# A GeGLU feed-forward by seven block products per pair of tiles, its down sums and residual rows in DRAM, and row-tiled state products in HGRN2

## What is computed

```python
h = rms_norm(x, norm_mix_pre)
proj = h @ w_in + b_in                      # 2048 x 11272
y_a = hgrn2_mix(...)                        # gated linear recurrence, 8 heads of 128, chunks of 64
y_b = mlstm_mix(...)                        # matrix memory, 4 heads
merged = sigmoid(gate_a) * (y_a @ w_up_a) + sigmoid(gate_b) * (y_b @ w_up_b)
x = x + rms_norm(merged @ w_out, norm_mix_post)
h = rms_norm(x, norm_ffn_pre)
gate = causal_dwconv(h @ ffn_w_gate, ffn_conv_w, ffn_conv_b)     # 2048 x 5632, three taps in time
up = h @ ffn_w_up                                                # 2048 x 5632
ffn_out = (gelu(gate, approximate=True) * up) @ ffn_w_down       # 5632 x 2048
x = x + rms_norm(ffn_out, norm_ffn_post)
```

## Time and profile before

| | |
|---|---|
| median of 3 runs | 2930.51 us (2930.03 to 2930.74) |
| the profiled execution | 2930.79 us, span of its core 2929.1 us |
| PE / PEld / DVE / ACT / POOL busy | 2886.0 / 2399.9 / 1149.2 / 823.2 / 87.8 us |
| granted TensorE clock | 0.996 of 2.4 GHz in the mean |
| DMA | 309 MB, mean 106 GB/s |

### The profile page before, as it was taken

The page is one execution under the profiler, slowest core; times in us unless marked ns, Lnnn a source line. Parts: engine busy times, 40 slices in busy tenths (PEclk is TensorE's granted clock), DMA queues, the critical chain, the costliest instruction groups (busy, mean ns, idle before and its releaser), DMA issues.

```text
span 2929.1 us, 32534 instructions
## 1 busy us (share of the span) xinstructions
PE 2886.0 (99%) x13167; PEld 2399.9 (82%) x13167; DVE 1149.2 (39%) x1141; ACT 823.2 (28%) x741; POOL 87.8 (3%) x99
## 2 busy tenths in 40 slices
PE   7999999999999999999999999999999999999997
PEld 6888888888888888888888888888888888888886
DVE  4232343344333234432554343343434343443436
ACT  3243434332222222222432222222221222122224
POOL 1000001000000000000000000000000000000004
PEclk9999999999999999999999999999999999999999
DMA  4323223332332334434333332333233233323334
GB/s 182 89 87 111 86 90 96 109 100 86 101 90 83 99 94 155 138 129 172 129 90 97 101 100 86 100 100 94 92 100 100 92 94 100 100 91 95 100 94 165
DMA packets 402657, 309.16 MB, mean 106 GB/s; under 512 B 5662, under 2 KB 349858, under 8 KB 401072
## 3 DMA queue, kind: packets, MB, share of 16 engines
q1 hardware_dynamic: 393824, 283.13, 31.0%
q0 software_dynamic: 4176, 16.95, 1.6%
q10 hardware_dynamic: 4608, 8.39, 0.7%
HBM read 295.87 MB, written 12.58 MB: 105 GB/s over the span
## 4 chain that ended last, share of the span: by engine, by line
PE 95%; DVE 2%; ACT 1%; POOL 1%; issue 0%; DMA 0%; DVEq 0%; SPq 0%; ACTq 0%
PE ps L657 21%; PE ps L386 18%; PE ps L660 11%; PE ps L389 9%; PE ps L405 7%; PE ps L407 7%; PE ps L406 7%; PE ps L603 6%; PE ps L679 1%; PE ps L678 1%; PE ps L677 1%; DVE w_lo L1126 1%; ACT w_hi L707 0%; PE ps L623 0%; DVE arena L1147 0%; PE ps L522 0%
## 5 line engine op out<-in xcount | busy, mean ns | idle before, releaser
L1126 DVE TENSOR_TENSOR w_lo<-raw,w_hi 128x2048 fp32r<-128x2048 f32 x260 | 597.1, 2297 | 1031.5 <-ACT w_hi L707 1031.5
L707 ACT CAST w_hi<-raw 128x2048 fp32r<-128x2048 f32 x260 | 496.3, 1909 | 615.9 <-PE ps L407 483.0
L657 PE MATMUL ps<-h_hi,w_hi 128*128 128x512 f32 x1376 | 325.9, 389 | 0.0
L657 PE MATMUL ps<-h_lo,w_hi 128*128 128x512 f32 x1376 | 325.9, 389 | 0.0
L660 PE MATMUL ps<-h_hi,w_lo 128*128 128x512 f32 x1376 | 325.9, 389 | 0.0
L657 PEld LDWEIGHTS ps<-h_lo,w_hi 128*128 128x128 f32 x1376 | 258.3, 188 | 53.6
L660 PEld LDWEIGHTS ps<-h_hi,w_lo 128*128 128x128 f32 x1376 | 258.3, 188 | 53.6
L657 PEld LDWEIGHTS ps<-h_hi,w_hi 128*128 128x128 f32 x1376 | 258.2, 188 | 53.6
L386 PE MATMUL ps<-h_hi,w_hi 128*128 128x512 f32 x1152 | 281.2, 397 | 1.1 <-ACT w_hi L707 1.1
L389 PE MATMUL ps<-h_hi,w_lo 128*128 128x512 f32 x1152 | 272.8, 389 | 0.0
L386 PE MATMUL ps<-h_lo,w_hi 128*128 128x512 f32 x1152 | 272.8, 389 | 0.0
(11 more groups left out here) (259 smaller groups left out, 2468.9 us busy)
## 6 DMA issues: line engine op xcount, KB each, us to landing
raw<-in_w_in SPq DMA_DIRECT2D x88, 1024.0 KB, 5.0
raw<-in_ffn_w_down SPq DMA_DIRECT2D x48, 1024.0 KB, 4.9
raw<-in_ffn_w_gate SPq DMA_DIRECT2D x44, 1024.0 KB, 5.1
raw<-in_ffn_w_up SPq DMA_DIRECT2D x44, 1024.0 KB, 5.1
raw<-in_w_out SPq DMA_DIRECT2D x20, 1024.0 KB, 4.9
merge_gates<-arena ACTq DMA_DIRECT2D x32, 256.0 KB, 2.0
raw<-in_w_up_a SPq DMA_DIRECT2D x8, 1024.0 KB, 5.0
raw<-in_w_up_b SPq DMA_DIRECT2D x8, 1024.0 KB, 5.1
```

What stands on the lines that cost most here:

```text
L657: pe.matmul(ps[:, bank + s, :], w[0][:, j, :], k[:, j, :], start=(k is h_hi and j == 0), stop=False)
L707: act.copy(w_hi[:, s, :], raw[:, s, :]).then_inc(hi_ready, 1)
L1126: dve.tensor_tensor(w_lo[:, s, :], raw[:, s, :], f32(w_hi[:, s, :]), ALU.subtract).then_inc(lo_ready, 1)
```

## The change

**Gate and up.** The weight of two hidden tiles (256 units x 2048 inputs) is cut into four quarters of 128 units x 1024 inputs: A11, A12 (first tile; first and second half of the inputs), A21, A22. h is cut into four quarters of 1024 inputs x 256 tokens. Instead of eight quarter products, seven products of sums (Strassen) are made, in the order M4, M2, M3, M5, M1, M7, M6. Four of the weight operands are new sums made on POOL (`weight_sum`: A21+A22, A11+A12, A11+A22, A12-A22, each 128x1024), one on DVE (`sum6`: A21-A11). All seven operands are then split into hi (ACT) and lo (DVE), each 128x1024, into a ring of three (`op_ring`). The seven operands of h are made once, ahead of the feed-forward: sums of token rows on DVE and POOL, 14 groups of 8 transposes (`turn_pieces`), and their split straight out of PSUM (`pieces_hi`, `pieces_lo`, 128x1024). In them hi and lo of 256 tokens stand side by side, so that one matmul of 512 columns makes w_hi*h_hi and w_hi*h_lo, and one of 256 columns w_lo*h_hi (`product`: 8 + 8 matmuls). Per pair of tiles the results are combined out of PSUM: three copies on ACT (`keep_product`), six additions of 128x512 on DVE (`with_m2` to `with_m6`, `from_m1`), four of 128x256 that join the two column halves (`both_halves`). The first tap moves from DVE to ACT.

**Loads.** Quarters of 512 KB go into a ring of six (`quad_ring`); a down block is two of them (`down(i, d, 0)` and `(i, d, 1)`, 24 matmuls each).

**Down sums.** The sums over the steps no longer lie in SBUF. ACT copies each 128x512 block out of PSUM (`down_copy`), and POOL issues a DMA that adds it to the tensor `down_sums` in DRAM (16 a step, `accum_op`; the first step writes). They are loaded back before the last down projection. `x1` too is stored to DRAM and loaded back for the last addition. The last step keeps the split of all its eight down operands for both halves of the tokens, where before the second half loaded and split them again.

**HGRN2.** The transposed keys of the two chunks lie in the two row halves of one tile (`hg_ket`, one copy on ACT in place of two, no zeroed padding), and the two state updates are matmuls over 64 rows each, issued in turns.

The core of the diff:

```diff
-            with pe.Fori(0, TT) as i:
+            for i in range(TT):
...
-                pe.wait_ge(k_end_copied, 2 * i + 2)
+                pe.wait_ge(k_end_copied, i + 1)
+                pe.wait_ge(hg_scores_copied, 2 * i + 2)
                 for h in range(HG_H):
-                    mm = pe.matmul(hT_[:, h, :], ke0[:, h, :], v_hg[:, ds(i, 1), h * P:(h + 1) * P], start=True, stop=True)
-                mm.then_inc(hg_update0, 1)
+                    m0 = pe.matmul(hT_[:, h, :], ket[0:CHUNK, h, :], v_hg[0:CHUNK, i:i + 1, h * P:(h + 1) * P],
+                                   start=True, stop=True)
+                    m1 = pe.matmul(hA_[:, h, :], ket[CHUNK:P, h, :], v_hg[CHUNK:P, i:i + 1, h * P:(h + 1) * P],
+                                   start=True, stop=True)
+                m0.then_inc(hg_update0, 1)
...
+            def product(i, p, q):
...
+                pe.wait_ge(ff_hi, o + 1)
+                for j in range(HALF):
+                    pe.matmul(ps[:, bank, :], w[0][:, j, :], h[:, j, :, :].rearrange("p r t -> p (r t)"),
+                              start=(j == 0 and q not in (M7, M6)), stop=False, skip_group_check=True)
+                pe.wait_ge(ff_lo, o + 1)
+                for j in range(HALF):
+                    mm = pe.matmul(ps[:, bank, 0:TH], w[1][:, j, :], h[:, j, 0, :], start=False, stop=(j == HALF - 1),
+                                   skip_group_check=True)
+                mm.then_inc(ff_op, 1)
...
+            def weight_sum(i, p, q):
...
+                if q == M2 or q == M5:
+                    before = o - PRODUCTS if p else o - OPS + 3 * PRODUCTS
+                    past(pool, ff_lo, before + (M1 if q == M2 else M7) + 1)
+                else:
+                    pool.wait_ge(ff_lo, o + (M2 if q == M1 else M5) + 1)
+                pool.tensor_tensor(dst, quads[(4 * p + a) % QRING], quads[(4 * p + b) % QRING],
+                                   ALU.subtract if q == M7 else ALU.add).then_inc(ff_sum, 1)
+
+            def sum_down(i, d, first):
+                for n in range(TT):
+                    pool.wait_ge(dn_evac, 16 * i + 4 * d + n + 1)
...
+                        pool.dma_start(dst, src, accum_op=ALU.add).then_inc(acc_added[n], 16)
...
+            def interval(i, k, with_lo=True):
...
+                if q == M2:
+                    with_m2(i, p)
+                elif q == M3:
+                    both_halves(i, p, X4)
+                    sum6(i, p)
+                elif q == M5:
+                    with_m5(i, p)
+                    both_halves(i, p, X3)
+                elif q == M7:
+                    with_m7(i, p)
+                    both_halves(i, p, X1)
+                    if up:
+                        times_gate(i, p, 0)
+                elif q == M6:
+                    with_m6(i, p)
+                    both_halves(i, p, Y2)
+                    if up:
+                        times_gate(i, p, 1)
+                    else:
+                        taps(i, p, 0)
+                    if p == 3:
+                        hidden_lo(i, p, 1)
+                if with_lo:
+                    lo(i, k + 2)
+                if q == M1:
+                    from_m1(i, p)
+                elif q == M7 and up:
+                    hidden_lo(i, p, 0)
+                elif q == M6 and p == 1:
+                    hidden_lo(i, p, 1)
+                elif q == M4 and up:
+                    taps(i, p - 1, 1)
```

More of the change, by code:

```diff
@@ L628, in _ @@
             for half, tiles in enumerate(HALVES):
                 for q in range(4):
+                    if half == 1 and q == 3:
+                        for r in range(4):
+                            turn_pieces(r)
                     u = U_OUT + 12 + 4 * half + q
@@ new lines, in ff_step, with need @@
+            def ff_step(i):
+                for p in range(PAIRS):
+                    for q in range(PRODUCTS):
+                        product(i, p, q)
+                for d in range(4):
+                    for h in range(2):
+                        down(i, d, h)
+            def need(count):
+                pe.wait_ge(th_lo, count)
+            need(2)
+            product(0, 0, M4)
+            need(4)
+            product(0, 0, M2)
+            for r in range(4, 8):
+                turn_pieces(r)
@@ L1078, in _, with row_power @@
             pool.dma_start(g_pre2, row_on_all(norm_ffn_pre, 0, D)).then_inc(x2_loaded, 16)
[L1080 removed]
+            def row_power(what, n):
                 if what == "mix":
@@ new lines, in _ @@
+            for n in range(2):
+                dve.tensor_tensor(x_rows[:, 2 + n, LEFT], x_rows[:, n, LEFT], x_rows[:, 2 + n, LEFT], ALU.add).then_inc(h_diff, 1)
+            lo(0, 5)
+            pieces_lo(10)
+            pieces_lo(11)
+            with_m5(0, 0)
+            dve.wait_ge(h_pool, 5)
+            dve.wait_ge(turned2, 8)
+            sum6(0, 0)
+            lo(0, 6)
+            pieces_lo(12)
+            lo(0, 7)
+            from_m1(0, 0)
+            pieces_lo(13)
+            both_halves(0, 0, X4)
```

796 lines of the change are left out of this document (577 added, 219 removed).

## The result

The changed kernel takes 2984.09 us (median of 4 runs, 2983.35 to 2985.36) against 2930.53 (2930.03 to 2930.74): a ratio of 1.0186, 95% interval 1.0174 to 1.0198, so 53.6 us slower. 2989 was forecast.

What follows compares the result with a forecast made beforehand. PE bounded the kernel before; after the change DVE, held up by POOL's sums, was to make PE wait in gate and up. From 2930.8: +46 (eleven steps) +17 (entry) -5 (HGRN2) = 2989 us, range 2850 to 3060.

Steps and rivals of the forecast that it cites:

- PE after the change: Feed-forward step: 2.77 us a product, 77.6 for 28, 121.1 us a step with the down part.
- Rival 4: Gate and up: 256-column matmuls wait for weight loads, so the change takes no PE time away; no chance given.
- DVE after the change: Step, from lo of operand 3 to last `hidden_lo`: 72.0 us; by itself DVE fits, 114.0 below 121.1.
- POOL holds DVE as a whole instruction: Gate and up: two-SBUF-input DVE instructions and POOL's exclude each other as wholes; at most 2.04 us a sum.
- 13 sums that the forecast counted: POOL sums in DVE's counted stretch of a step: holds of 20.7 us, making the step 134.7 us.
- A sign that did not come: Gate and up: POOL sums of 2.3 us stretched to 3 to 4.5.
- hold by M5's sum: Step: three M5 sums, somewhere between `with_m5` and `from_m1`, hold DVE 0 to 2.1 us each, 1.0 taken.
- Rival 2: Steps: holds of about 1.0 a sum, M5's perhaps beside `from_m1` and `with_m7`; 127.0 a step, 2904 us; chance 0.15.
- Entry: Feed-forward entry: DVE and POOL add 12 to 30 us, 2 are PE idle time; 17 taken (8 to 28).
- HGRN2, -5: HGRN2 row tiles: half-row updates save 7 us in all if halves run at once, else none; -5 taken.
- End: From 2868.5 us: kept splits save DVE work, second down half waits about 6 us for `hidden_lo`; even.
- rival 3: Gate and up: PE's clock falls too; at 0.75 a product takes 3.7 us, +7 a step, 3066 us; chance 0.10.

## Why the prediction came out right

By its own steps:

- **PE after the change, 121.1 a step.** Right: 121.73 with POOL's sums cut to 8 columns. A product of 2.77 is 2.79 in the trace. Rival 4 (weight loads) is out.
- **DVE after the change, 72.0 of own work.** 69.3 in the step shown: from the lo of operand 3 (1910.59) to the end of the last `hidden_lo` (1999.44) it is 88.9 us, less 19.6 of holds. A little dear.
- **POOL holds DVE as a whole instruction.** Right, shown by doses: 25.5 us a step, 1.59 a sum. The 13 sums that the forecast counted, at 20.7 us, hold by 19.6 in the step shown (each instruction's length less what it takes unhurt); the other three hold more, among them 2.5 us at 1906.97. By the figure of the Trainium skill ("GPSIMD Engine Reference", Elementwise — side-by-side cycle accounting) the estimate for a sum was 2.35 us; the trace agrees, its shortest takes 2.34.
- **A sign that did not come.** POOL's sums of 3 to 4.5 us: they stayed at 2.3 to 2.9. The exclusion works both ways (4.32 us at 1440.27), but the forecast did not see that most sums start just behind a lo part and so ask first.
- **The mis-sized terms of a step.** The hold by M5's sum first: the prediction took 1.0 and named 0 to 2.1. In the step shown A12 lands at 1923.17, in time for the sum to run beside `from_m1` and `with_m7`, and 0.2 is left. Three times 0.8 is 2.4. The other ten sums hold by 19.0 where 17.7 was taken, +1.3; DVE's own work is 2.7 less; and its way starts 5.5 us into the step, not 3.9, +1.6. The second down half starts 94.4 us into a step, not 96.6, and a step is 132.6, not 134.7. Over the ten steps between first down halves that is +22.1 in place of +41; the eleventh lies in the end. Rival 2's mechanism was real for this one sum of four.
- **Entry, +17 (8 to 28).** Wrong: 35.5, outside its own bounds. The step reckoned DVE's added work and holds as so many us, "2 are idle time of PE and the rest is spread". What the rows show in its place, from the first turn to the first down half, first before and then after the change:

```profile
1453.88:1563.10 109.22, 104.07 (x570) 90.09 (x569) 55.09 (x56) 38.38 (x45) 2.24 (x5) 0.98 0.31 97
1448.03:1592.73 144.70, 109.45 (x585) 94.27 (x584) 127.32 (x115) 63.52 (x77) 54.27 (x26) 0.87 0.29 90
```

PE idles 35.3 us in place of 5.2, +30.1: 24.4 more up to the dense part at 1527.10, and 5.7 behind it for lo parts. Its busy time grows by 5.4. In that, 48 more turned blocks cost about 5 us (eight take 0.81 at the full level, 1515.59 to 1516.40), and the products save 10.2 (28 x 2.79 for 288 x 0.2267 + 192 x 0.120, the matmuls of that gate and up part before). So some 10 us are left, an estimate, and the rows put them to the clock: eight blocks take 1.76 us at 1455.40, after PE's idle 6.33 us, in place of 0.81, and the granted clock is 0.76 up to the dense part.

Holds are part of it: the entry is 7.0 us shorter with 8-column sums in all pairs but the first and 13.2 shorter with copies in all. Moving the first pair's sums to DVE brought nothing, nor did reordering. The rest is a chain. The two norms and row differences that 14.0 us are waited for existed in the kernel before as norms, and PE then had 17.2 us of ready matmuls (1458.56 to 1475.77) where it now has 12.7 (1461.35 to 1474.08): of Strassen's products two can run on the first two row tiles, the third needs the last two, and the fifth sums of all four.

- **HGRN2, -5.** -5.8 in both traces that have it.
- **End, "even".** +2.9. From the last step's first down half to PE's last product it is 50.7 us, where 192 matmuls need 43.5: the wait before the second down half is 4.68 us (about 6 was forecast), and the granted clock is 0.93 over the stretch. The forecast's eleventh step, 4.1 us, belongs here. With 8-column sums the wait is 2.43 us and the end 60.8, even with the kernel before; with 768 columns the wait is 4.68 and the end 64.4, so it doesn't follow the dose in proportion, and why stays open.
- **Clock (rival 3).** No fall in gate and up of the steady steps: 1.00 in the stretch shown, with PE waiting between products by up to 1.8 us. The Trainium skill ("TensorE: Matmul & The Clock Gate", A second HAM failure mode: psum-queue depth-cycling) tells of a kernel whose clock swung because PE idled briefly and often between groups of matmuls. By that the clock would swing here, and in these stretches the trace does not agree. It does fall in the entry, at about 10 us by the estimate above, which the forecast had left out there.

So the total is right by 5 us, with the ten steps too dear by 19 and the entry too cheap by 18. That these cancel is luck. The mechanism in the steps was right and the sizes in it near; in the entry the holds were seen, and the chain that leaves PE idle and the clock that falls with it were missed.

What stays open: whether sums placed on purpose beside additions out of PSUM would be free on POOL (that order wasn't tried); how the entry's idle time divides between the holds and the chain, since copies shorten both; and the clock's share there, which is a remainder.

## What to carry to other kernels

Work given to an idle GpSimd is not free when VectorE works from SBUF beside it: here each sum of 1024 columns took 1.6 us from VectorE and cost it 1.1 to 1.2 when it did the sum itself. Before moving work there, multiply the count by the hold, and see which instructions of VectorE would stand under it; here additions out of PSUM could, lo parts could not. When an arithmetic saving on TensorE shifts the load, price the other engine's whole list first: 2.5 us more of matmuls a step, which spared VectorE 11.6 (96.48 to 84.91), were the better trade. And an algorithm whose third product needs the last inputs loses the overlap at its entry, once; the three orders of instructions run there did not bring it back. Idle time of PE cost twice there: behind waits of 4 us and more the matmuls ran in part at the lower clock, some 10 us in all by the estimate above.
